# Turning the softmax blocks of two attentions with VectorE squares and a DRAM exchange instead of TensorE transposes

## What is computed

```python
def _mem_attention(q, mem, w_mem_kv):
    k, v = jnp.split(mem @ w_mem_kv, 2, axis=-1)
    ...
    p = jax.nn.softmax(sc, axis=-1).astype(vh.dtype)
    return jnp.einsum('bhqk,bhkd->bhqd', p, vh)

def _causal_attention(q, k, v):
    ...
        sc = jnp.where(kpos[None, :] <= qpos[:, None], sc, -jnp.inf)
        p = jax.nn.softmax(sc, axis=-1).astype(v.dtype)
        return jnp.einsum('bhqk,bhkd->bhqd', p, v)

def _layer(x, mem, positions, w_in, ...):
    (r_q, r_k, r_v, a_cq, ..., c_q, z) = _split_cols(x @ w_in, IN_SPLITS)
    ...
    y = jnp.concatenate([ret, mla, mls, memo], axis=-1) * jax.nn.silu(z.astype(f32))
    y = y.astype(x.dtype) @ w_out
    return _layernorm(DEEPNORM_ALPHA * x + y, ln_g, ln_b)
```

## Time and profile before

| | us |
|---|---|
| median of 3 runs (lowest, highest) | 906.46 (905.54, 906.92) |
| the profiled execution's own time | 907.26 |
| its span, first to last instruction | 905.4 |
| PE busy / weight loads busy | 899.3 / 781.5 |
| DVE busy | 654.7 |
| ACT busy | 493.6 |

### The profile page before, as it was taken

One profiled execution on the slowest core, in us unless ns is written; L12 is line 12 of the kernel. 1 busy time (PEld: TensorE's weight loads), 2 busy tenths in 40 slices (PEclk: granted clock), 3 DMA queues, 4 the chain that ended last, 5 costly groups with the idle time before them and its releaser, 6 DMA issues.

```text
span 905.4 us, 13911 instructions
## 1 busy us (share of the span) xinstructions
PE 899.3 (99%) x4872; PEld 781.5 (86%) x4872; DVE 654.7 (72%) x1294; ACT 493.6 (55%) x934; POOL 16.0 (2%) x18
## 2 busy tenths in 40 slices
PE   9999999999999999999999999999999999999997
PEld 8888998888888888888888889888888888888896
DVE  6868776877775775666669787778777667787865
ACT  6665765645545455644476657746354544555551
POOL 0000000000000000000000000000000000000001
PEclk9999999999999999999999999999999999999999
DMA  9785456645874475656654865585475754766832
GB/s 358 270 320 163 133 173 232 186 142 176 276 250 162 162 225 197 206 187 196 199 187 140 306 222 157 174 245 165 137 232 163 232 166 162 231 189 233 338 102 93
DMA packets 58132, 183.03 MB, mean 202 GB/s; under 512 B 6856, under 2 KB 12240, under 8 KB 57424
## 3 DMA queue, kind: packets, MB, share of 16 engines
q1 hardware_dynamic: 57488, 181.10, 61.0%
q10 hardware_dynamic: 576, 1.05, 0.3%
HBM read 174.78 MB, written 7.35 MB: 201 GB/s over the span
## 4 chain that ended last, share of the span: by engine, by line
PE 98%; issue 1%; DMA 0%; ACT 0%; POOL 0%; DVE 0%; POOLq 0%; ACTq 0%; DVEq 0%
PE acc L1330 23%; PE acc L1315 18%; PE acc L1316 18%; PE acc L1319 18%; PE acc L1336 12%; PE work L1044 1%; PE work L1051 1%; PE work L1050 1%; PE work L1049 1%; PE work L1214 1%; PE work L1213 1%; DMA B<-in_mem_t 0%; PE work L1242 0%; PE work L1230 0%; PE work L1145 0%
## 5 line engine op out<-in xcount | busy, mean ns | idle before, releaser
L1402 DVE TENSOR_TENSOR lo<-raw,hi 128x512 fp32r<-128x512 f32 (+2 forms) x607 | 387.6, 657 | 204.3 <-ACT hi L1008 190.9
L1008 ACT ACTIVATE hi<-raw 128x512 fp32r<-128x512 f32 (+2 forms) x607 | 351.4, 603 | 270.0 <-PE acc L1319 143.1
L1315 PE MATMUL acc<-hi,xx 128*128 128x512 f32 (+2 forms) x576 | 213.4, 374 | 0.0
L1316 PE MATMUL acc<-hi,xx 128*128 128x512 f32 (+2 forms) x576 | 209.0, 366 | 0.0
L1330 PE MATMUL acc<-xx,hi 128*128 128x512 f32 x768 | 193.5, 394 | 0.0
L1319 PE MATMUL acc<-lo,xx 128*128 128x512 f32 (+2 forms) x576 | 164.3, 366 | 0.0
L1330 PEld LDWEIGHTS acc<-xx,hi 128*128 128x128 f32 x768 | 138.2, 189 | 24.9
L1316 PEld LDWEIGHTS acc<-hi,xx 128*128 128x128 f32 x576 | 108.6, 189 | 16.0
L1315 PEld LDWEIGHTS acc<-hi,xx 128*128 128x128 f32 x576 | 108.6, 189 | 16.1
L1319 PEld LDWEIGHTS acc<-lo,xx 128*128 128x128 f32 x576 | 104.3, 188 | 17.7 <-DVE lo L1402 0.3
L1336 PEld LDWEIGHTS acc<-xx,lo 128*128 128x128 f32 x768 | 104.8, 190 | 7.6
(11 more groups left out here) (347 smaller groups left out, 1041.1 us busy)
## 6 DMA issues: line engine op xcount, KB each, us to landing
raw<-in_w SPq DMA_DIRECT2D x263, 512.0 KB, 3.9
raw<-in_w SPq DMA_DIRECT2D x26, 256.0 KB, 2.7
raw<-in_w SPq DMA_DIRECT2D x16, 328.0 KB, 3.1
B<-turn SPq DMA_DIRECT2D x40, 128.0 KB, 3.7
turn<-B SPq DMA_DIRECT2D x6, 512.0 KB, 5.5
Y<-in_wuq SPq DMA_DIRECT2D x2, 1152.0 KB, 7.4
Y<-in_x_t SPq DMA_DIRECT2D x4, 512.0 KB, 9.0
X<-in_x SPq DMA_DIRECT2D x4, 512.0 KB, 6.5
```

Source lines behind the costliest of these rows:

```text
L1008: act.activation(place(l, t, hi), raw[:, s, (t % 2) * w:(t % 2 + 1) * w], ACT.Copy)\
L1315: pe.matmul(o, ah[:, q], hi[:, s, 0:w], start=k == 0, stop=False, skip_group_check=name == "memv")
L1316: pe.matmul(o, al[:, q], hi[:, s, 0:w], start=False, stop=False, skip_group_check=name == "memv")
L1402: dve.tensor_tensor(place(l, t, lo), raw[:, s, (t % 2) * w:(t % 2 + 1) * w], place(l, t, hi).bitcast(F32), ALU.subtract).then_inc(lo_done. ...
```

## The change

The transposes `mem_pT` and `mla_pT` leave PE. DVE instead transposes 32x32 squares of each head (`turn_head`: two instructions of 128x256 for mem, one of 128x384 for mla), and SP sends two heads at a time through DRAM and back. `mem_pTh`/`pTl` are then split from the buffer that came back; mla's product reads its buffer directly, so ACT's copy to `probT` is gone. The steps around them move: `mem_out` on PE from slots 92 and 105 to 100 and 108, `mla_out` from 174 and 186 to 182 and 192, DVE's copies of them from 99 and 110 to 104 and 113 and from 179 and 191 to 187 and 197. Some buffers get another place, and the four loads of `x` in layer 0 go from pairs 80, 84, 88, 92 to 97, 99, 101, 103.

```diff
--- before.py
+++ after.py
-    _put(PE_AT, (78, 84, 91, 98)[_h], "mem_pT", _h)
-    _put(PE_AT, 162 + 6 * _h, "mla_pT", _h)
-        (92, "mem_out", 0), (105, "mem_out", 1),
+        (100, "mem_out", 0), (108, "mem_out", 1),
-        (174, "mla_out", 0), (186, "mla_out", 1),
+        (182, "mla_out", 0), (192, "mla_out", 1),
-    _put(ACT_AT, 84 + 6 * _h + _h // 2, "mem_pT", _h)
+    _put(ACT_AT, (96, 97, 104, 105)[_h], "mem_pT", _h)
-    _put(ACT_AT, 167 + 6 * _h, "mla_pT", _h)
-    _put(DVE_AT, 85 + 6 * _h + _h // 2, "lo", "mem_pT", _h)
+    _put(DVE_AT, (79, 83, 93, 95)[_h], "turn_head", "mem", _h)
+    _put(DVE_AT, (97, 98, 105, 106)[_h], "lo", "mem_pT", _h)
+    _put(DVE_AT, 161 + 6 * _h, "turn_head", "mla", _h)
...
-TURNS = ("c", "cell", "rq", "rk", "ret")
-TURN_OUT_AT = {57: "c", 77: "cell", 81: "rq", 89: "rk", 112: "ret"}
-TURN_IN_AT = {59: "c", 79: "cell", 83: "rq", 91: "rk", 114: "ret"}
+TURNS = ("c", "cell", "rq", "rk", "ret", "mem0", "mem1", "mla0", "mla1")
+TURN_COLS = {n: 3 * HEADS * P // 2 if n[:3] == "mla" else 4 * SEQ for n in TURNS}
+TURN_OUT_AT = {46: "mem0", 51: "mem1", 57: "c", 77: "cell", 81: "rq", 88: "mla0", 89: "rk", 93: "mla1", 112: "ret"}
+TURN_IN_AT = {49: "mem0", 53: "mem1", 59: "c", 79: "cell", 83: "rq", 90: "mla0", 91: "rk", 95: "mla1", 114: "ret"}
...
                     if m == 57:
                         sp.wait_ge(mrow_out.sem, mrow_out.at(l, 0))
-                        wait_job(sp, l, ("mem_out", 1))
+                        sp.wait_ge(pt_split.sem, pt_split.at(l, 3))
...
                         if name == "mem_pT":
-
-                            wait_job(act, l, (name, i), *([("mem_out", 0)] if i >= 2 else []))
+                            wait_turned(act, l, f"mem{i // 2}")
+                            if i >= 2:
+                                wait_job(act, l, ("mem_out", 0))
...
                 def mem_out(q):
                     wait_acc_read(pe, l, CI["memv"])
-                    wait_read(pe, l, ("mem_pT", 2 * q), ("mem_pT", 2 * q + 1))
+                    pe.wait_ge(pt_split.sem, pt_split.at(l, 2 * q + 1))
...
                 def mla_out(q):
-                    wait_read(pe, l, ("mla_v", 0), ("mla_v", 1), ("mla_pT", 2 * q), ("mla_pT", 2 * q + 1))
+                    wait_read(pe, l, ("mla_v", 0), ("mla_v", 1))
+                    wait_turned(pe, l, f"mla{q}")
...
+                def turn_head(name, h):
+
+                    dve.wait_ge(prob_done.sem, prob_done.at(l, h + (HEADS if name == "mla" else 0)))
+                    if (name, h) == ("mem", 0):
+                        wait_job(dve, l, ("ml_fold", 0))
+                    group = f"{name}{h // 2}"
+                    if name == "mem":
+                        src = prob[:, h % 2, :].rearrange("p (i k n) -> p k i n", i=NT, k=2)
+                        dst = squares[group].rearrange("p (b g k i r) -> p g k i b r", b=4, g=2, k=2, i=NT)[:, h % 2]
+                        for k in range(2):
+                            m = dve.transpose(dst[:, k], src[:, k].rearrange("p i (b c) -> p i b c", b=4))
+                    else:
+                        m = dve.transpose(squares[group].rearrange("p (b g n r) -> p g n b r", b=4, g=2, r=32)[:, h % 2],
+                                          prob[:, h % 2, 0:TRI].rearrange("p (n b c) -> p n b c", n=3, b=4))
+                    m.then_inc(squared[group].sem, 1)
```

More of the change, by code:

```diff
@@ L496, in build_trunk @@
         roped = signal("roped", 4)
-        squared = {n: signal(f"squared_{n}", 1) for n in TURNS}
+        squared = {n: signal(f"squared_{n}", 2 if n[:3] in ("mem", "mla") else 1) for n in TURNS}
+        pt_split = signal("pt_split", 4)
         turn_out = {n: signal(f"turn_out_{n}", 1, step=16) for n in TURNS}
@@ L616, in operand @@
             if name == "mem_pT":
-                return bank(l, (name, i)), pTh[:, i % 2, :], pTl[:, i % 2, :], free_bank(l, name, i)
+                h, rest = (x[:, i % 2, :].rearrange("p (n a r) -> p n a r", n=4, a=4) for x in (pTh, pTl))
+                return turned_head("mem", i), h, rest, pt_split.sem
             return A(l, "memv", i), mV[0][:, i, :], mV[1][:, i, :], acc_sem(l, "memv")
@@ L700, in _ @@
                         name = TURN_OUT_AT[m]
[L701 to L702 removed]
+                        sp.wait_ge(squared[name].sem, squared[name].at(l, squared[name].per_layer - 1))
+                        sp.dma_start(a["turn"][TURNS.index(name), :, 0:TURN_COLS[name]], squares[name]).then_inc(turn_out[name].sem, 16)
                     if m in TURN_IN_AT:
@@ L883, in mla_exp @@
                     e.then_inc(exp_done.sem, 1)
-                def mla_pT(h):
-                    wait_job(act, l, ("mla_pT", h), *([("mla_out", 0)] if h >= 2 else []))
-                    act.activation(probT[:, h % 2, 0:TRI], bank(l, ("mla_pT", h))[:, 0:TRI], ACT.Copy)\
-                       .then_inc(free_bank(l, "mla_pT", h), 1)
                 def silu_conv(q):
@@ L1215, in mla_scores @@
                     m.then_inc(job_done.sem, 1)
-                def mla_pT(h):
-                    pe.wait_ge(prob_done.sem, prob_done.at(l, HEADS + h))
-                    o = take("mla_pT", h)
-                    for j in range(3):
-                        m = turn(o[:, j * P:(j + 1) * P], prob[:, h % 2, j * P:(j + 1) * P])
-                    m.then_inc(job_done.sem, 1)
                 def mla_out(q):
-                    wait_read(pe, l, ("mla_v", 0), ("mla_v", 1), ("mla_pT", 2 * q), ("mla_pT", 2 * q + 1))
+                    wait_read(pe, l, ("mla_v", 0), ("mla_v", 1))
+                    wait_turned(pe, l, f"mla{q}")
                     stand_alone(pe)
@@ L1228, in mla_out @@
                     for h in (2 * q, 2 * q + 1):
-                        c = (h % 2) * 256
-                        pe.matmul(o[:, c:c + 256], mlaV[:, 0, h * HD:(h + 1) * HD], probT[:, h % 2, 0:256],
-                                  start=True, stop=False, skip_group_check=True)
-                        m = pe.matmul(o[:, c + P:c + 256], mlaV[:, 1, h * HD:(h + 1) * HD], probT[:, h % 2, 256:TRI],
+                        to = o[:, (h % 2) * 256:(h % 2 + 1) * 256].rearrange("p (i a r) -> p i a r", i=NT, a=4)
+                        pt = turned_head("mla", h)
+                        pe.matmul(to, mlaV[:, 0, h * HD:(h + 1) * HD], pt[:, 0:2], start=True, stop=False, skip_group_check=True)
+                        m = pe.matmul(to[:, 1], mlaV[:, 1, h * HD:(h + 1) * HD], pt[:, 2],
                                       start=False, stop=True, skip_group_check=True)
@@ L1520, in evacuate @@
                         wait_job(dve, l, (name, q))
+                        if name == "mem_out":
+                            dve.wait_ge(turn_out["mem1"].sem, turn_out["mem1"].at(l, 0))
                         dve.tensor_copy(dst[:, 2 * q:2 * q + 2, :], bank(l, (name, q)).rearrange("p (j t) -> p j t", j=2))\
@@ L1596, in gates @@
                     wait_job(dve, l, ("gateT", 0), ("ml_fold", 0))
+                    dve.wait_ge(turn_out["mem0"].sem, turn_out["mem0"].at(l, 0))
                     dve.wait_ge(cols_in.sem, cols_in.at(l, 0))
```

54 lines of the change are left out of this document (28 added, 26 removed).

## The result

| | before | after |
|---|---|---|
| median (lowest, highest), us | 906.16 (905.54, 906.92) | 914.93 (914.14, 915.99) |
| profiled execution's own time / span | 907.26 / 905.4 | 914.14 / 912.3 |

The ratio is 1.0102, with a 95% interval of 1.0090 to 1.0113: the change makes the kernel 8.8 us slower. I had forecast +3.4 us (909.9, range 904 to 914). The direction was right, the size was not, and the time lies outside my range.

The account below looks back on a forecast made before the run. PE was taken to bound the kernel on average, with DVE and ACT choking it at slots 99 and 171. Mem parts of 2.4 and 2.1 us and mla's -1.1 gave +3.4, 909.9 us on the median; range 904 to 914.

Parts of the forecast that it names:

- The choke at slot 99: PE only just not late for DVE's lo at slot 99: margins 0.06 us in layer 0, 0.28 in layer 1.
- rival A: Whole kernel: PE's count of work decides, so all 6.2 us come off, 900.3 us; chance 0.14.
- DVE's squares: Ahead of slot 99: a mem head's pair of square transposes takes DVE 0.7 us, making gates and lo about 1.0 late.
- `mem_out` behind the choke: Slot 100: the first pair's twelve matmuls, moved from slot 92 to behind slot 99, add 1.42 us a layer.
- rival B: Slot 99: idle time absorbs the added squares, the moved mem_out still costs; -0.1 us, 906.4; chance 0.2 with nearby mixtures.
- The read-back of mem0: Before ACT's split at slot 96: data land at 126.3 to 129, costing nothing up to 128.8.
- rival C: Slots 97 and 98: mem0 lands at 131 or 132, 2 to 3 us later still a layer, 914 to 916; chance 0.08.
- its sign: At ACT: being seen waiting on turn for long would show the forecast wrong; no size given.
- The mla part: Slots 161 to 171: transposes removed, -1.32 us, less 0.76 of waiting, gives -0.56 a layer.
- its choke is at slot 171: Head 1's squares delay the maximum of mla head 2 and hi of slot 171 by 0.5 us; margin 0.4.
- Nothing is given back: Behind slot 100: PE is over 2 us later and DVE about 1, so margins grow and no time returns.

Follow-up runs that it names:

- short_out0: Kernel before, with two of the twelve matmuls of the first pair's mem_out ahead of slot 99 kept in each layer: 905.71 against 905.77 us, ratio 0.9996.
- scan_2more: Kernel before, with the first scan of gate_scan done three times instead of once: 908.08 against 905.48 us, ratio 1.0031.
- late_split: Changed kernel, with the first pair's splits moved to slots 99 and 100 and mem_out to 102, second pair one slot later: 907.88 against 905.77 us.
- early_read: Changed kernel, with the read-back of the first pair's squares issued behind weight pair 48 instead of 49: 911.25 against 905.62 us before.
- fill: Changed kernel, with 5, 12 and 15 extra matmuls, results thrown away, behind slots 96, 97 and 98: 914.45 against 905.95 us before.
- mla_spread: Kernel before with the mla part alone, head 1's squares and rk's turn moved to slot 171: 904.55 against 905.48 us, ratio 0.9986.
- loose: Changed kernel, with softplus, splits, gate_scan, gate_floor, gate_cols and mem_out around slot 99 moved to later slots: 906.13 against 905.48 us before.
- the best version: Changed kernel, with the chain around slot 99, the readers of mrow, mla steps and first two mem heads' squares moved: 903.21 against 905.58 us before.
- scan_6more: Kernel before, with the first scan of gate_scan done seven times instead of once: 11.5 us slower, ratio 1.0127.
- no_return: Changed kernel, with the first mem pair's splits reading a constant instead of the returned exchange: 4.1 us slower than before, ratio 1.0046.

## Why the prediction was off, step by step

- **The choke at slot 99** (margins of 0.06 and 0.28 us, of which the hand-over takes 0.06): right. short_out0 and scan_2more show it from both sides, and rival A, the count of PE's work, falls with it.
- **DVE's squares**: right in size. The pair of head 2 stands between 123.41 and the next instruction at 124.09, so it holds DVE for 0.68 us (I took 0.7):

```profile
123.41 0.77 DVE L1508 STREAM_TRANSPOSE B<-prob 128x256 f32<-128x256 f32 x2
124.09 0.46 DVE L1397 TENSOR_TENSOR lo<-raw,hi 128x328 fp32r<-128x328 f32 x1
```

  `gates` starts at 126.86, aligned 128.88, against 128.19 before: 0.7 us late, not 1.0. With an early read-back `lo` of slot 99 is 0.66 and 0.93 us late against the 1.0 of the sum.
- **`mem_out` behind the choke**, +1.42 us a layer: right, and the largest term that I had; late_split is left with hardly anything else. The mem part of rival B, in which the squares cost nothing (1.36 and 1.14 us), comes close to the 1.5 and 1.6 of late_split.
- **The read-back of mem0 is "covered, narrowly"**: this step failed. I put its cost at nothing; it was 3.6 us. In layer 0 the data were read at 130.0 aligned where the deadline was 128.8. I had the four reads issued by about 124; the last one went out at 124.8 and took 5.19 us, inside the 2.7 to 5.3 us that I quoted. In layer 1, on the scale of layer 0, it went out at 124.3 and took 6.88 us, outside of them, and was read at 131.2. So in layer 0 the later issue did more than the landing, in layer 1 the landing. That spread was of all 40 reads of the kernel before, none of which lies in this stretch. It is the last of the four that counts, and it is the slowest of its four in all ten turns there, with 3.6 to 5.3 us; here it took 5.2 and 6.9 us, in early_read 5.7 and 5.5, in fill 7.6 and 5.7. And I judged the room by the queue's mean of 61%. In the stretch of the exchange the DMA share was 0.47 and 0.71 before and is 0.89 and 0.93 now, as the first two rows (before) and the last two (after, about the same stretch when aligned) show:

```profile
123.00:128.00 5.00, 5.00 (x37) 4.82 (x36) 3.12 (x9) 4.21 (x11) 0.00 (x0) 1.00 0.47 157
128.00:133.00 5.00, 5.00 (x33) 4.70 (x32) 2.81 (x7) 3.97 (x8) 0.00 (x0) 1.00 0.71 252
...
121.00:126.00 5.00, 5.00 (x36) 4.85 (x35) 3.47 (x12) 3.62 (x10) 0.00 (x0) 1.00 0.89 233
126.00:131.00 5.00, 4.07 (x19) 2.84 (x17) 3.42 (x8) 2.98 (x5) 0.00 (x0) 1.00 0.93 308
```

This was my rival C, "2 to 3 us later still in each layer", to which I gave 0.08. By early_read it is 1.3 us in layer 0 (1.94 - 0.66) and 2.3 in layer 1 (3.00 - 0.71). That the time itself, 914.93, falls into its 914 to 916 is luck in part: 3.6 us come from the read-back, and 2.0 by the trace from the clock, which that rival did not have. I had also named its sign, ACT seen waiting on `turn` for long: 2.82 and 3.85 us. For a transfer whose deadline, 128.8, lies inside the spread of arrivals that I had worked out, 126.3 to 129, with a queue ahead of it, 0.08 was too little, and the range should have taken in all of this rival. The Trainium skill (DMA: Bandwidth & Descriptors, Latency and other measured facts) lets the latency of the memory grow with its load, up to 2 us; the rows agree in direction, with landings of 5.2 to 6.9 us at a share of 0.9. The warning of the Trainium skill (Perfetto Trace Analysis, DMA Optimizations) of transfers under 2 KB, which I had cited, is not told apart from the load by any run here.
- **The clock**: missing from the sum. I had no row with a low clock in the kernel before, and so no term for it: 1.6 + 0.4 us in the profiled execution.
- **The mla part**, -0.56 forecast, -0.44 and -0.45 in the trace: right. That its choke is at slot 171 is right too, but it is not the only one: behind it stands slot 177, which took 0.5 us back in mla_spread.
- **Nothing is given back** behind slot 100: right for the changed kernel, whose margins there grew as I wrote (`lo` of slot 101 is 3.9 us ahead of PE, 0.9 before). loose shows why one must not conclude from this that the places behind are free.

Of the 5.5 us between forecast and trace, 3.3 are the wait at slot 99 (the read-back 3.6, the squares 0.3 less than forecast), 2.0 the clock and 0.2 mla.

## What to carry to other kernels

When work leaves the bound engine by way of DRAM, draw up the deadline of the transfer and the spread of landings in that very stretch, with the new transfers in it; if they overlap, put the reader behind whatever chain runs there, which cost nothing here and was worth 6.7 us. Price a wait of TensorE at more than its length, since it can be followed by a stretch at half clock. And where PE is bound and others follow it closely, look for the choke behind the one that you open: with slots 99, 112 and 171 cleared, others (0.3 us a layer ahead of slot 88, more at 101 to 108 and at 177) still took back 3.8 of the 6.2 us that the best version saves on PE.

## What the runs showed of the hardware that I had not expected

- Granted clock behind short waits. In the changed kernel no single gap of PE was longer than 1.9 us in layer 0 (0.80, 1.42 and 1.88 us, with work between them), and the clock fell to 0.50, the 1.2 GHz level, for 3.4 us. One gap of about 1.1 us (scan_2more) left it at 1.00, as did two of 1.3 us (late_split), one of 4.2 and 3.9 us (scan_6more) lowered it each time, and filling the gap with matmuls whose result nobody reads kept it at 1.00. The Trainium skill (TensorE: Matmul & The Clock Gate, Part 1: The HAM clock gate) says that this clock follows how busy the engine has lately been; the fill runs agree.
- Near this border it is a matter of luck: in early_read layer 0 pays 1.6 us for waits (1.28 and 1.86 us) that cost layer 1 (1.25 and 1.99 us) nothing, and in no_return it is the other way round; of its six executions three show no fall.
- The landing of the same read-back, with the same issue order, came 1.8 us later in layer 0 and 1.1 us earlier in layer 1 of fill than in the changed kernel. One must not rely on a landing to a microsecond at a DMA share of 0.9.
